# Another order of the first layer's attention units, with the output units starting on the other half of K

## The chip, the cores and the metric

The kernel runs on one core of a Trainium2 chip. The metric is the time on the device in microseconds. Three runs of the kernel before took 2024.71 to 2028.53 us, median 2028.3 us. The engines are named as in the profile: PE is TensorE's matmul stream, DVE is VectorE, ACT is ScalarE, POOL is GpSimd and SP is SyncE, which issues nearly all transfers.

## The reference, cut to what matters

Two transformer layers on 256 tokens of width 2048, all in float32. The change touches the first layer's attention only:

```python
proj = h @ w_in                      # h: modulated norm of x; 3904 columns
dq, dk, dv, q_lat, kv_lat, k_pe = split(proj, (1024, 1024, 1024, 512, 256, 64))
o_diff = diff_attention(rope(dq), rope(dk), dv, lam)      # 8 heads, two softmaxes each
o_diff = rmsnorm(o_diff, g_diff_sub) * (1 - lambda_init)
q  = rmsnorm(q_lat) @ w_q_b;  kv = rmsnorm(kv_lat) @ w_kv_b
o_mla = mla_attention(q, kv, rope(k_pe))                  # 8 heads, one softmax each
x = x + gate_m * (concat([o_diff, o_mla]) @ w_out)
h = modulate(rmsnorm(x, g_norm_ffn), shift_f, scale_f)    # then the feed-forward part
```

The shifts, scales and gates are `silu(c) @ w_ada + b_ada`, a product of one row with a matrix of 2048 x 12288.

## The kernel before, in words

**Units and pairs.** Every large product is cut into units of 512 (or 384, 320) output columns, and a unit into pairs of K tiles (2 x 128 rows). One pair is one transfer of 512 KB into one of five `raw` slots, a rounded copy by ACT (`whi`, line 1685), a remainder by DVE (`wlo`, line 1897), and 12 matmuls on PE: eight with `whi` (lines 1550 and 1551) and four with `wlo` (line 1555). Sums of a unit stand in two of four PSUM banks `g`. `run` (line 522) writes the pairs and prepares weights three pairs ahead; `whi` and `wlo` have four buffers each.

**The dots.** The product with `w_ada` is not on PE: DVE multiplies a tile of 512 KB with the row and sums it (line 1902, "dot" below). The tiles come through the same five slots. `fill` (line 457) puts a dot into the program wherever its planner, a table of assumed durations, sees DVE with time to spare. After the attention two more slots are added.

**The attention.** The first halves of K of the six `w_in` units have been computed and parked in `part` (in the tensor `region`) before the latent columns. Then the loop at line 1069 runs through the table `order1` (line 604). An entry `("h", i)` is the second half of K of unit i (0, 1: queries; 2, 3: keys; 4, 5: values), four pairs; `half_unit` (line 1033) adds the parked part on DVE. An entry `("l", i)` is `latent_units` (line 1043): two pairs for the queries and one for keys and values of latent heads 2i and 2i+1. Heads are generators in a queue `bg`: `diff_head` (line 825) and `mla_two` (line 897, two latent heads, scores of both together). Up to four of them are advanced between the pairs. A differential head 0 to 3 needs units 0, 2 and 4, a head 4 to 7 needs units 1, 3 and 5.

**What comes out.** Finished heads are normalised and turned into the K tiles of the output product: `mla_end(p)` (line 983) makes one K pair of two latent heads, `diff_end(j)` (line 881) two K pairs of four differential heads, after an inverse root by 11 small DVE instructions. The rows of `w_out` are rolled on the host, so that K tiles 0 to 7 belong to the latent heads and 8 to 15 to the differential ones. The latent K tiles take the place of the latents and can be written only when the last latent unit is done. `diff_end` is put into the queue behind everything else, after the loop. `spread` (line 640) makes the gate's rows.

**The output units.** `u_out[0]` and `u_out[1]` run their first four pairs, then `u_out[0]` its other four (lines 1105 to 1107); then the queue is drained, and `u_out[1]`, `u_out[2]`, `u_out[3]` follow, 32 pairs in all. `reload` (line 1097) has POOL load x (2.1 MB) when the queue is empty. The products are multiplied by the gate on DVE (line 2110) and added to x. The feed-forward part starts with an inverse root over all of x and matmuls at line 1581.

Of the kernel before, what the change touches and what calls it, by code (L numbers as in the profile page):

```python
# [152 lines left out]
def program(nc, a, out):  # L153
    with ExitStack() as ctx:
        build(nc, ctx, a, out)


def build(nc, ctx, a, out):
    def sb(name, shape, dt=F32, scope=ctx):
        return scope.enter_context(nc.sbuf_tensor(name, shape, dt))  # L160
# [8 lines left out]
    lhsA = Lhs(sb("lhsA_hi", [P, 16, 256], F32R), sb("lhsA_lo", [P, 16, 256], F32R), 16)  # L169
# [53 lines left out]
    region = sb("region", [P, 11264], F32, early)  # L223
# [4 lines left out]
    lamv = rowv[:, 0:256].rearrange("p (a b) -> p a b", a=4)  # L228
    red = [region[:, 10784:10864], region[:, 10864:10944]]
    gt = region[:, 0:2048]  # L230
    part = [region[:, 1024 * i:1024 * i + 1024].rearrange("p (t d) -> p t d", t=2) for i in range(6)]
    omla = region[:, 2048:4096].rearrange("p (t d) -> p t d", t=2)
    odiff = [region[:, 4096 + 1024 * j:5120 + 1024 * j].rearrange("p (t d) -> p t d", t=2) for j in range(2)]
    vm = region[:, 6144:8192].rearrange("p (t d) -> p t d", t=2)
# [58 lines left out]
    def mark(kind):  # L293

        engine, s = signal[kind]
        count[kind] = count.get(kind, 0) + 1
        latest[engine] = (s, count[kind])
        return latest[engine]

    def fence():  # L300
        return list(latest.values())
# [62 lines left out]
    def tile_of(name, k, c0):  # L364
        at, n = tile_at(name, ROWS.get(name, D), k, c0)
        return a[name][at:at + 2 * P * n].rearrange("(p x) -> p x", p=P)

    def units(us, row=0, native=False):
        built = []
        for w, c0, n, K, lhs in us:  # L370
            k_off, K = K if isinstance(K, tuple) else (0, K)
            u = dict(n=n, K=K, lhs=lhs, tiles=[], k_off=k_off, pairs=list(range(K // 2)))
            for k0 in range(0, K, 2):
                u["tiles"].append(len(plan))
                plan.append((tile_of(w, row + k_off + k0, c0), n, native))
            built.append(u)
        return built
# [4 lines left out]
    pairs, used_up, fetched = {}, {}, {}  # L382
# [103 lines left out]
    def pump(n=1, width=2, idle=False):  # L486
        for _ in range(n):
            fill()
            moved, again = False, True
            while again:  # L490
                again, live = False, 0
                for g in list(bg):
                    if live < width or g in started:
                        started.add(g)
                        live += 1
                        if soon(g, SLACK):
                            again = advance(g) or again
                moved = moved or again
            if idle and not moved:
                held = [g for g in bg if g in started and waiting.get(id(g))]  # L500
                held.sort(key=lambda g: max([due[m] for m in waiting[id(g)][1]] + [0.0]))
                for g in held:
                    if advance(g):
                        break
# [96 lines left out]
    u_h0 = units([("w_in", 512 * i, 512, (0, 8), lhsA) for i in range(6)])  # L601
    u_lat = units([("w_in", 3072, 512, 16, lhsA), ("w_in", 3584, 320, 16, lhsA)])
    u_in, u_q = {}, []
    order1 = (("h", 2), ("h", 3), ("l", 0), ("h", 0), ("l", 1), ("h", 4), ("l", 2), ("l", 3), ("h", 1), ("h", 5))
    for kind, i in order1:
        if kind == "h":
            u_in[i], = units([("w_in", 512 * i, 512, (8, 8), lhsA)])
        else:
            u_q.extend(units([("w_q_b", 384 * i, 384, 4, lhs_q), ("w_kv_b", 512 * i, 512, 2, lhs_kv)]))
    u_out = units([("w_out", 512 * i, 512, (0, 8), lhsA) for i in range(2)])  # L610
    for u, v in zip(u_out, units([("w_out", 512 * i, 512, (8, 8), lhsA) for i in range(2)])):
        u["tiles"], u["pairs"] = u["tiles"] + v["tiles"], list(range(8))
    u_out += units([("w_out", 512 * i, 512, 16, lhsA) for i in range(2, 4)])
    u_f1, u_f2 = [], []
    for g in range(4):
# [190 lines left out]
    def latents_turned():  # L806
        for p in range(3):
            b = take(SB)
            lhs, c0, k0 = (lhs_q, V_QA + 2 * p, 2 * p) if p < 2 else (lhs_kv, V_KVA, 0)
            tok = turned(b, blocks_of(lat, (2 * p * P, 2 * p * P + P)), t_of["lat", 0], t_of["lat", 512])  # L810
            split_from(b, tok, 2, [vec[:, c0 + i:c0 + i + 1] for i in range(2)], lhs, k0, *lhsA.free, t_vec)
# [171 lines left out]
    def mla_end(p):  # L983
        while any(("omla", h) not in t_of for h in (2 * p, 2 * p + 1)):
            yield
        yield "pe", [t_of["omla", 2 * p], t_of["omla", 2 * p + 1]]
        T = yield from grab(TOB)
        tok = turned(T, blocks_of(omla, (2 * p * P, 2 * p * P + P)), t_of["omla", 2 * p], t_of["omla", 2 * p + 1])
        yield "act", [tok]
        split_from(T, tok, 2, ONE, lhsA, 2 * p, t_of["latents"])  # L990
# [42 lines left out]
    def half_unit(i):  # L1033
        if i < 4:
            got = run(u_in[i], width=4)
            r = take(rows)
            bg.append(g_qk(r, sum_parts(got, i, r.ap, *r.after), qT if i < 2 else kT, 4 * (i % 2),
                           0.125 if i < 2 else 1.0, ("qT" if i < 2 else "kT", i % 2)))
        else:
            j = i - 4  # L1040
            note(("dv", j), sum_parts(run(u_in[i], width=4), i, dv[:, :, 512 * j:512 * j + 512], *stage))

    def latent_units(i):
        r, ks = row_unit(u_q[2 * i], width=4)
        bg.appendleft(g_q(r, ks, i))
        par, tok = run(u_q[2 * i + 1], steps=2, width=4)
        r = take(rows)
        got = [G[2 * par + t].rearrange("p (s w) -> p s w", w=256) for t in range(2)]
        ks, kv = mark("evac"), mark("evac")
        step("evac", [(r.ap[:, t, 0:256].rearrange("p (s w) -> p s w", w=P), got[t][:, :, 0:P], 1.0) for t in range(2)],  # L1050
             tok, r.after, ks)
        step("evac", [(vm[:, t, 256 * i:256 * i + 256].rearrange("p (s w) -> p s w", w=P), got[t][:, :, P:2 * P], 1.0)
                      for t in range(2)], tok, stage, kv)
        gfree[par] = [kv]
        note(("vm", i), kv)
        bg.appendleft(g_kv(r, ks, i))
        bg.append(mla_two(i))
# [10 lines left out]
    halved = set()  # L1068
    for kind, i in order1:
        if kind == "h":  # L1070
            half_unit(i)
            halved.add(i)
            if i == 1:
                gate_free = [latest["pe"], latest["act"], latest["dve"]]
            for j in range(2):
                if i in (j, 2 + j, 4 + j) and {j, 2 + j, 4 + j} <= halved:
                    for h in range(4 * j, 4 * j + 4):
                        bg.append(diff_head(h))
        else:
            if i == 0:  # L1080
                while counts.get("lat", 0) < 2:
                    pump(1, 4, True)
                latents_turned()
                stage = fence()
            latent_units(i)
            if i == 3:
                lhsA.ready[0:4] = [None] * 4
                t_of["latents"] = latest["pe"]
                for p in range(4):
                    bg.append(mla_end(p))  # L1090
# [387 lines left out]
    for j in range(4):  # L1478
        y = take(ys)
        for b in range(3):  # L1480
# [5 lines left out]
            u, k0 = u_br[j, b], br_at[b]  # L1486
# [20 lines left out]
    for j in range(4):  # L1507
        par, tok = run(u_o2[j])
        t = mark("rows_out")
# [864 lines left out]
```

## Time and profile before

| | |
|---|---|
| three runs | 2024.71, 2028.53, 2028.3 us |
| profiled execution | 2027.03 us, its span 2025.2 us |
| busy in the span | PE 95%, DVE 65%, ACT 46%, POOL 6% |
| granted clock, whole span | 0.98 |
| loop over `order1` and output units | about 219 to 496 us of the span |

A matmul's end is modelled in these profiles, so a time for several matmuls is best read from start to start. Where rows follow each other without idle time, their durations overlap a little; two dots in a row take 2.3 us, not 2.44.

### The profile page before, as it was taken

How to read it: one execution, taken by the hardware profiler on the slowest of the kernel's cores; microseconds unless marked ns; L12 is line 12 of the kernel's file. 1: busy time of each engine (PE TensorE's matmuls, PEld its weight loads, DVE VectorE, ACT ScalarE, POOL GpSimd, SP SyncE). 2: the span in 40 equal slices, each digit the busy share in tenths (PEclk: the TensorE clock that was granted, in tenths of full speed). 3: DMA queues.
4: the chain of work that ended last, by engine and by line, in shares of the span. 5: the costliest groups of instructions: out<-in, count | busy, mean ns of one | idle time of the engine just before them, and what ended most of it. 6: DMA issues, size and time to landing. Idle time of an engine off the chain costs nothing.

```text
span 2025.2 us, 24834 instructions
## 1 busy us (share of the span) xinstructions
PE 1930.6 (95%) x9250; PEld 1608.7 (79%) x9250; DVE 1308.6 (65%) x2056; ACT 941.6 (46%) x1437; POOL 129.7 (6%) x94
## 2 busy tenths in 40 slices
PE   6699999778899999999999999989999999999999
PEld 3278788556788888888888889889998888888887
DVE  3788888979788555555555556668666555555554
ACT  2455466524544344344434454456455544444442
POOL 0000000001000110110010022010000010100000
PEclk9899999889899999999999999999999999999999
DMA  9998686878799555555555545534545465655644
GB/s 348 368 391 339 232 282 215 292 255 326 274 321 319 196 206 186 191 188 189 186 196 187 187 167 198 189 113 158 170 151 180 147 205 190 191 190 189 198 178 176
DMA packets 128968, 448.83 MB, mean 222 GB/s; under 512 B 14288, under 2 KB 14544, under 8 KB 128336
## 3 DMA queue, kind: packets, MB, share of 16 engines
q1 hardware_dynamic: 124928, 433.74, 61.5%
q0 software_dynamic: 1568, 7.34, 1.0%
q10 hardware_dynamic: 2352, 6.17, 0.8%
q8 instruction: 73, 1.20, 0.2%
q14 instruction: 47, 0.39, 0.1%
HBM read 443.00 MB, written 4.19 MB: 221 GB/s over the span
## 4 chain that ended last, share of the span: by engine, by line
PE 90%; DVE 5%; DMA 2%; issue 1%; ACT 1%; POOL 0%; ACTq 0%; SPq 0%; DVEq 0%; POOLq 0%
PE g L1550 27%; PE g L1555 27%; PE g L1551 27%; PE pT L1574 1%; DVE raw L1902 1%; PE g L1566 1%; PE pS L1574 1%; DMA region<-in_mem 1%; PE pO L1626 1%; DMA raw<-in_w_ada 1%; DVE wlo L1897 1%; PE pT L1587 0%; PE pS L1644 0%; DMA raw_wide<-in_w_ada 0%; PE pS L1594 0%
## 5 line engine op out<-in xcount | busy, mean ns | idle before, releaser
L1897 DVE TENSOR_TENSOR wlo<-raw,whi 128x1024 fp32r<-128x1024 f32 (+3 forms) x553 | 659.2, 1198 | 519.4 <-ACT whi L1685 486.6
L1685 ACT ACTIVATE whi<-raw 128x1024 fp32r<-128x1024 f32 (+3 forms) x553 | 554.7, 1007 | 663.7 <-PE g L1555 572.3
L1550 PE MATMUL g<-whi,lhsA_hi 128*128 128x512 f32 (+4 forms) x1840 | 701.1, 383 | 40.0 <-issue 14.6
L1551 PE MATMUL g<-whi,lhsA_lo 128*128 128x512 f32 (+4 forms) x1840 | 687.9, 376 | 0.0
L1555 PE MATMUL g<-wlo,lhsA_hi 128*128 128x512 f32 (+4 forms) x1840 | 465.2, 375 | 3.2 <-DVE wlo L1897 3.1
L1550 PEld LDWEIGHTS g<-whi,lhsA_hi 128*128 128x128 f32 x1840 | 349.7, 190 | 98.7 <-issue 37.6
L1551 PEld LDWEIGHTS g<-whi,lhsA_lo 128*128 128x128 f32 x1840 | 350.1, 190 | 51.6 <-issue 0.5
L1555 PEld LDWEIGHTS g<-wlo,lhsA_hi 128*128 128x128 f32 x1840 | 339.4, 190 | 58.4 <-DVE wlo L1897 3.7
L1550 PE MATMUL g<-whi,lhsF_hi 128*128 128x512 f32 x512 | 200.9, 392 | 0.0
L1551 PE MATMUL g<-whi,lhsF_lo 128*128 128x512 f32 x512 | 199.4, 389 | 0.0
L1902 DVE SCALAR_TENSOR_TENSOR raw<-raw,srow 128x1024 f32<-128x1024 f32 x145 | 174.8, 1227 | 6.6 <-DMA raw<-in_w_ada 6.3
L1897 DVE TENSOR_TENSOR wlo<-region,whi 128x1024 fp32r<-128x1024 f32 (+1 forms) x99 | 122.8, 1248 | 85.8 <-ACT whi L1685 77.1
L1685 ACT ACTIVATE whi<-region 128x1024 fp32r<-128x1024 f32 (+1 forms) x99 | 102.1, 1036 | 124.1 <-PE g L1555 121.1
L1555 PE MATMUL g<-wlo,lhsF_hi 128*128 128x512 f32 x512 | 137.0, 390 | 0.0
L1555 PEld LDWEIGHTS g<-wlo,lhsF_hi 128*128 128x128 f32 x512 | 96.2, 188 | 20.1
L1550 PEld LDWEIGHTS g<-whi,lhsF_hi 128*128 128x128 f32 x512 | 96.2, 188 | 19.9 <-issue 0.2
L1551 PEld LDWEIGHTS g<-whi,lhsF_lo 128*128 128x128 f32 x512 | 96.2, 188 | 19.7 <-issue 0.2
L2287 POOL TENSOR_TENSOR region<-region,tmp 128x512 f32<-128x512 f32 x36 | 60.6, 1705 | 700.2 <-DVE tmp L2110 689.4
L1550 PE MATMUL g<-whi,lhsY_hi 128*128 128x512 f32 x128 | 50.2, 392 | 0.0
L1551 PE MATMUL g<-whi,lhsY_lo 128*128 128x512 f32 x128 | 49.9, 390 | 0.0
L1550 PE MATMUL g<-whi,yz_hi 128*128 128x512 f32 x128 | 49.8, 389 | 0.0
L1551 PE MATMUL g<-whi,yz_lo 128*128 128x512 f32 x128 | 49.8, 389 | 0.0
(265 smaller groups left out, 1497.7 us busy)
## 6 DMA issues: line engine op xcount, KB each, us to landing
raw<-in_w_ff SPq DMA_DIRECT2D x185, 512.0 KB, 4.2
raw<-in_w_in SPq DMA_DIRECT2D x159, 512.0 KB, 4.2
raw<-in_w_ada SPq DMA_DIRECT2D x145, 512.0 KB, 5.3
region<-in_w_ff SPq DMA_DIRECT2D x71, 512.0 KB, 4.3
raw<-in_w_out SPq DMA_DIRECT2D x60, 512.0 KB, 5.4
raw<-in_w_in SPq DMA_DIRECT2D x80, 384.0 KB, 3.1
region<-in_w_ada SPq DMA_DIRECT2D x36, 512.0 KB, 6.0
region<-in_w_in SPq DMA_DIRECT2D x17, 512.0 KB, 10.1
```

The source lines that it names most:

```text
L1550: eng.matmul(o, p.xh[:, kk, t * P:t * P + P], h, start=p.first and kk == 0, stop=False)
L1551: eng.matmul(o, p.xl[:, kk, t * P:t * P + P], h, start=False, stop=False)
L1555: ins = eng.matmul(p.banks[t][:, 0:n], p.xh[:, kk, t * P:t * P + P], p.lo[:, kk * n:kk * n + n], start=False, stop=p.last and kk == 1)
L1566: ins = eng.matmul(p.banks[t][:, 0:n], p.xh[:, kk, t * P:t * P + P], p.raw[:, kk * n:kk * n + n], start=p.first and kk == 0, stop=p.last a ...
L1574: ins = eng.transpose(b.ap[:, i * P:i * P + P], src, ident)
L1626: ins = eng.matmul(o[:, dh * r:dh * r + dh], pt[:, 256 * i + P * r:256 * i + P * r + P], vals[:, i, v0:v0 + dh], start=i == 0, stop=i == 1)
L1685: eng.activation(p.hi, p.raw, ACT.Copy).then_inc(p.hi_done[0], 1)
L1897: eng.tensor_tensor(p.lo, p.raw, p.hi.bitcast(F32), ALU.subtract).then_inc(p.lo_done[0], 1)
L1902: eng.scalar_tensor_tensor(out=x, in0=x, scalar=0.5, in1=srow[:, D // 2 * (i % 2):D // 2 * (i % 2) + D // 2], op0=ALU.mult, op1=ALU.mult, ...
L2287: eng.tensor_tensor(xc, xc, tm[:, :], ALU.add).then_inc(t[0], 1)
```

## The change

The table `order1` is another one: differential heads 0 to 3 have their last unit third (`h` 2) instead of sixth, heads 4 to 7 theirs eighth (`h` 3) instead of tenth, and latent units 2 and 3 come last. The parked parts change places in `region`, so that the two that lie where the gate's rows go (parts 5 and 3) are used up when `gate_free` is taken. Units 0 and 1 of the output product begin with K tiles 8 to 15 (differential) and end with 0 to 7 (latent); the other two are as before.

```diff
-    part = [region[:, 1024 * i:1024 * i + 1024].rearrange("p (t d) -> p t d", t=2) for i in range(6)]
+    part = [region[:, 1024 * i:1024 * i + 1024].rearrange("p (t d) -> p t d", t=2) for i in (3, 5, 4, 1, 2, 0)]
...
-    order1 = (("h", 2), ("h", 3), ("l", 0), ("h", 0), ("l", 1), ("h", 4), ("l", 2), ("l", 3), ("h", 1), ("h", 5))
+    order1 = (("h", 4), ("h", 0), ("l", 0), ("h", 2), ("l", 1), ("h", 1), ("h", 5), ("h", 3), ("l", 2), ("l", 3))
...
-    u_out = units([("w_out", 512 * i, 512, (0, 8), lhsA) for i in range(2)])
-    for u, v in zip(u_out, units([("w_out", 512 * i, 512, (8, 8), lhsA) for i in range(2)])):
-        u["tiles"], u["pairs"] = u["tiles"] + v["tiles"], list(range(8))
+    u_out = units([("w_out", 512 * i, 512, (8, 8), lhsA) for i in range(2)])
+    for u, v in zip(u_out, units([("w_out", 512 * i, 512, (0, 8), lhsA) for i in range(2)])):
+        u["tiles"], u["pairs"], u["k_off"] = u["tiles"] + v["tiles"], [4, 5, 6, 7, 0, 1, 2, 3], 0
...
-            if i == 1:
+            if {3, 5} <= halved and i in (3, 5):
                 gate_free = [latest["pe"], latest["act"], latest["dve"]]
```

PE's program shows what the planner makes of it at the end of the attention. In the kernel before, this is what follows the first four pairs of `u_out[0]` and of `u_out[1]`: the last three differential heads (pT from `probs` is a head's turned probabilities, pS its scores, pO its values), two steps of the gate's rows (`rot`), the first turned output of `diff_end` and the next pair of `u_out[0]`.

```order
L1594 MATMUL pS<-region 128x256 x4
L1626 MATMUL pO<-region,pt 128x128 x4
L1574 MATMUL pT<-cst,probs 128x128 x4
L1594 MATMUL pS<-region 128x256 x4
L1626 MATMUL pO<-region,pt 128x128 x4
L1574 MATMUL pT<-cst,probs 128x128 x4
L1587 MATMUL pT<-rot,cst 128x512
L1626 MATMUL pO<-region,pt 128x128 x4
L1574 MATMUL pT<-cst,probs 128x128 x4
L1587 MATMUL pT<-rot,cst 128x512
L1626 MATMUL pO<-region,pt 128x128 x4
L1574 MATMUL pT<-cst,region 128x128 x4
```

In the changed kernel the last pair of the last latent unit is followed by 32 such rows without one pair among them: four differential and four latent heads (the two rows at lines 1604 and 1609 are scores of two latent heads), and everything that ends them. These are the last twelve before the first pair of `u_out[0]`.

```order
L1626 MATMUL pO<-region,pt 128x128 x4
L1574 MATMUL pO<-cst,region 128x128 x4
L1574 MATMUL pT<-cst,probs 128x128 x8
L1626 MATMUL pO<-region,pt 128x128 x4
L1574 MATMUL pT<-cst,probs 128x128 x4
L1626 MATMUL pO<-region,pt 128x128 x8
L1574 MATMUL pT<-cst,region 128x128 x4
L1574 MATMUL pO<-cst,region 128x128 x4
L1587 MATMUL pT<-rot,cst 128x512
L1574 MATMUL pT<-cst,region 128x128 x4
L1574 MATMUL pO<-cst,region 128x128 x4
L1587 MATMUL pT<-rot,cst 128x512
```

What moved: in the kernel before, eight pairs of output units stand among the last eight heads, and four more among the rows of `diff_end`; now all 32 stand behind the heads.

On DVE, this stands in the kernel before around the splits of the differential K pairs (`lhsA_lo` with `vec`): dots at line 1902, the scaling by the norm at line 2071, one remainder at line 1897. The first of the four differential splits stands ahead of it.

```order
L1902 SCALAR_TENSOR_TENSOR raw,small<-raw,srow 128x1024 x3
L2071 TENSOR_TENSOR region<-region,small 128x512 x2
L1929 SCALAR_TENSOR_TENSOR lhsA_lo<-pO,vec,lhsA_hi 128x256 x2
L1937 TENSOR_SCALAR rot<-cst,small 128x128 x4
L1897 TENSOR_TENSOR wlo<-raw,whi 128x1024
L1902 SCALAR_TENSOR_TENSOR raw,small<-raw,srow 128x1024 x2
L1914 TENSOR_TENSOR mods<-small 128x4
L1917 TENSOR_TENSOR mods<-mods,vec 128x4
L1922 SCALAR_TENSOR_TENSOR mods<-mods,vec 128x4
L1929 SCALAR_TENSOR_TENSOR lhsA_lo<-pO,vec,lhsA_hi 128x256 x2
```

And this in the changed kernel, from the end of the second inverse root on:

```order
L1937 TENSOR_SCALAR rot<-cst,small 128x128 x4
L2071 TENSOR_TENSOR region<-region,small 128x512 x2
L1929 SCALAR_TENSOR_TENSOR lhsA_lo<-pT,vec,lhsA_hi 128x256 x2
L1929 SCALAR_TENSOR_TENSOR lhsA_lo<-pO,vec,lhsA_hi 128x256 x2
L1902 SCALAR_TENSOR_TENSOR raw,small<-raw,srow 128x1024 x4
L1937 TENSOR_SCALAR rot<-cst,small 128x128 x4
L1929 SCALAR_TENSOR_TENSOR lhsA_lo<-pO,vec,lhsA_hi 128x256 x2
L1929 SCALAR_TENSOR_TENSOR lhsA_lo<-pT,vec,lhsA_hi 128x256 x2
L1897 TENSOR_TENSOR wlo<-raw,whi 128x1024
```

What moved: both inverse roots and both scalings now stand ahead of the first of these splits, and behind all latent heads, because `diff_end` is queued last, although the outputs of differential heads 0 to 3 are complete long before. In the kernel before, the four latent K pairs were split first and had pairs of `u_out` behind them.

## Rows read from the trace of the kernel before

**Rows 1.** Stretches: length; busy PE, PEld, DVE, ACT, POOL; clock, DMA share, GB/s.

```profile
244.00:343.00 99.00, 99.00 (x551) 83.47 (x550) 83.15 (x167) 67.42 (x167) 0.00 (x0) 1.00 0.72 243
343.00:412.00 69.00, 54.31 (x274) 41.35 (x272) 64.52 (x152) 36.05 (x103) 0.00 (x0) 0.88 0.77 273
412.00:440.00 28.00, 19.47 (x62) 14.33 (x63) 24.88 (x54) 6.33 (x11) 0.84 (x1) 0.77 0.67 225
440.00:496.00 56.00, 55.59 (x243) 45.51 (x242) 47.97 (x64) 22.06 (x29) 10.67 (x6) 0.99 0.98 373
384.00:412.00 28.00, 18.52 (x78) 12.71 (x76) 24.70 (x69) 13.84 (x48) 0.00 (x0) 0.70 0.58 197
```

**Rows 2.** Waits of PE and of SP's queue, 343 to 441 us: total, times, longest.

```profile
PE g L1550 <- DVE lhsA_lo L1929: 10.1, 4, 4.5
SPq L1529 <- DVE raw L1902: 56.2, 35, 8.1
```

**Rows 3.** DVE's instructions by line, 343 to 412 us: count, busy us, mean ns, idle before.

```profile
L1902 DVE SCALAR_TENSOR_TENSOR raw<-raw,srow 128x1024 f32<-128x1024 f32 x24 | 28.8, 1219 | 0.3 <-DMA raw<-in_w_ada 0.3
L1897 DVE TENSOR_TENSOR wlo<-raw,whi 128x1024 fp32r<-128x1024 f32 x10 | 12.2, 1222 | 0.1
L1937 DVE TENSOR_SCALAR rot<-cst,small 128x128 f32<-128x128 f32 x12 | 2.6, 280 | 0.0
L1929 DVE SCALAR_TENSOR_TENSOR lhsA_lo<-pT,lhsA_hi 128x256 fp32r<-128x256 f32 x4 | 1.5, 418 | 0.0
L2071 DVE TENSOR_TENSOR region<-region,small 128x512 f32<-128x512 f32 x2 | 1.3, 686 | 0.0
L2104 DVE TENSOR_TENSOR region<-g,region 128x512 f32<-128x512 f32 x2 | 1.3, 684 | 0.0
```

**Rows 4.** PE in order of time: start us, us, instruction, idle time before it.

```profile
342.16 1.07 PE L1555 MATMUL g<-wlo,lhsA_hi 128*128 128x512 f32 x4
343.95 1.89 PE L1604 MATMUL pS<-region 128*128 128x256 f32 x8
345.78 1.14 PE L1609 MATMUL pS<-hn_sq,region 64*128 64x256 f32 x8
...
390.68 2.09 PE L1594 MATMUL pS<-region 64*128 64x256 f32 x8
...
412.10 0.47 PE L1550 MATMUL g<-whi,lhsA_hi 128*128 128x512 f32 x1 [2.07 <-DVE lhsA_lo L1929]
...
416.14 1.42 PE L1587 MATMUL pT<-rot,cst 128*128 128x512 f32 x2
...
440.93 0.39 PE L1550 MATMUL g<-whi,lhsA_hi 128*128 128x512 f32 x1
...
505.12 1.20 PE L1581 MATMUL pS<-region 128*128 128x128 f32 x4 [9.54 <-issue]
```

**Rows 5.** The chain that ended last: start us, us, what (three dots with their reads).

```profile
364.48 3.44 DVE raw L1902 x6
```

**Rows 6.** DVE in order of time: an inverse root, and a late dot.

```profile
403.39 0.16 DVE L1860 TENSOR_SCALAR small<-small 128x8 f32<-128x8 f32 x1
...
405.39 0.17 DVE L1872 SCALAR_TENSOR_TENSOR small<-small 128x8 f32<-128x8 f32 x1
...
497.38 1.23 DVE L1902 SCALAR_TENSOR_TENSOR raw<-raw,srow 128x1024 f32<-128x1024 f32 x1 [2.12 <-DMA raw<-in_w_ada]
```

**Rows 7.** Transfers from 440 to 497.4 us: packets, bytes, mean rate.

```profile
DMA packets 5649, 21.45 MB, mean 374 GB/s; under 512 B 611, under 2 KB 611, under 8 KB 5455
```

**Rows 8.** Transfers' size and median us to landing, 343 to 412 us.

```profile
raw<-in_w_out SPq DMA_DIRECT2D x9, 512.0 KB, 5.2
```

**Rows 9.** The same from 420 to 450 us.

```profile
raw<-in_w_out SPq DMA_DIRECT2D x5, 512.0 KB, 8.7
```

**Rows 10.** POOL in order of time: the load of x, and what waited for it.

```profile
436.23 0.84 POOL L2276 DMA_DIRECT2D region<-in_x  x1 [435.79 <-DVE lhsA_lo L1929]
447.86 3.61 POOL L2287 TENSOR_TENSOR region<-region,tmp 128x512 f32<-128x512 f32 x2 [10.78 <-DMA region<-in_x]
```

## The prediction, made before the changed kernel was run

> **What bounds the kernel now.** I read the stretches first, then the waits in the one that is not full, then DVE's groups, then the transfers. [rows 1] show three regimes around the change. From 244 to 343 us PE is busy throughout at full clock (2.4 GHz, granted 1.00) while DVE has 16 us to spare of 99: PE is the bound, and moving work about gives nothing there. From 343 to 440 us PE has holes and a lower clock, while DVE is busy 64.5 of 69 us and 24.9 of 28: DVE is the bound. SP's queue waits for DVE as well, because each dot holds a slot [rows 2]. From 440 to 496 us PE is full again, with the transfers at 98%: the bound is PE with the transfers right behind it. The proof of "right behind" is the last dot before the final gate product, which sat 2.1 us for its data at 497.4 us, when PE had been done since 495.6 (505.12 less 9.54) [rows 4, 6].
>
> So the question is what the change does to the middle regime, and whether the third one can still follow.
>
> **Start of the tail.** In the kernel before, the last pair of the last attention unit ends at 343.1 us (the first row of [rows 4] with what lies behind it). In the changed kernel the same number of pairs stands ahead of the last latent unit's end. Of the other PE work, one step of scores of two latent heads (343.95 to 346.9 us, 2.9 us [rows 4]) and two turned outputs (0.44 us each at full clock) are not ahead any more, and one differential head's scores more are (2.09 us at half clock, so about 1.05). PE was the bound there, so this counts: 343.1 - 2.9 - 0.9 + 1.1 = 340.4 us.
>
> **The tail without pairs.** In both kernels eight heads are unfinished at that point. Before, eight pairs stood among them and the first pair that needs a differential split began at 412.1 us [rows 4]. Now none stands among them, so PE is free; but PE was not the bound. I take DVE's work of 343 to 412 us and change what the order changes: 64.5 us; ten remainders were in it, one is now (9 x 1.15 = 10.3 less); 24 dots, now 23 (1.15 less); 12 rows of `rot`, now 8 (0.8 less); the parked sum and one rope (2.4 less); one inverse root more (403.39 to 405.39 and its last instruction, 2.1) and one scaling (1.2) [rows 3, 5, 6]; splits and output copies, 0.5 more. That is 53.6 us, and 1.1 for the first scores, 54.7. A dot is 1.15 from start to start (3.44 for three [rows 5]).
>
> To this come DVE's own waits. Before they were 4.5 us in 69 (69 less 64.5), with six of the last eight heads under cover of other DVE work. Now the last four heads are latent, scored two at a time, and DVE stands behind a chain: maximum, exponential on ACT, turn, copy, values, output, turn, split, and each only when the one bank for turns is free again. From 384 to 412 us, where heads ran without pairs, the clock was 0.70, mostly at 1.2 GHz, and DVE was busy 24.7 of 28 [rows 1]. At full clock I count three such stops, 8 us in all; at 1.2 GHz the two steps of latent scores cost 5.8 instead of 2.9 us each and the turns and values double, 14 us. I take 11, nearer to neither, since the clock was mixed. The first output pair then begins at 340.4 + 54.7 + 11 = 406.1 us, with 4.5 and 14 as bounds: 400 to 409.
>
> Before it began at 412.1; so the tail is about 6 us shorter. But before, twelve pairs were done or under way by 440 us, eight of them in this stretch. Now all 32 stand behind it.
>
> **The 32 output pairs.** The undisturbed pace: from 440.93 to 495.6 us there are 20 pairs, 2.73 us each [rows 4]. The first twelve (units 0 and the half of 1, on five slots): 12 x 2.73 = 32.8; two turned outputs of `diff_end(1)`, 0.9; two steps of `rot`, 1.7; a first pair that begins in the low clock, 1.3 (412.10 to 416.14 us is 4.0 [rows 4]). Then the load of x. It is 2.1 MB, 5.6 us at the 374 GB/s of [rows 7]. Before, it was issued at 436.2 and landed at 447.9 us [rows 10], and weights took 8.7 us to land around it instead of 5.2 [rows 8, 9]; PE did not feel it, since it had been slow just before and three prepared pairs were waiting. Now it falls after about the sixth of 32 pairs in a row, with DVE just ahead of PE (11 remainders and 18 dots belong to these twelve pairs, 33 us, with splits and `rot` 39 us against PE's 37). I put 3 of the 5.6 us on the path; the bounds are 0 and 5.6. Sum 39.7: unit 0 ends at 445.8 us. Then 20 pairs as before, 54.6, and 1 us because they start with empty slots: 501.4 us.
>
> The transfers by themselves: 62 tiles for remainders and dots, three for the next stage, less five in the slots, is 60 x 0.524 MB, with x 33.6 MB, 90 us at 374 GB/s [rows 7]. 406 + 90 = 496 us. They can follow, but with 5 us in 95 to spare, which is why a lost microsecond is not given back.
>
> The Trainium skill, DMA: Bandwidth & Descriptors, section Issuing engines are not separate DMA queues, says that transfers started by any engine run on the same 16 DMA engines and interleave. Here the trace agrees: the load of x goes through POOL, and the weights of SP's queue landed 3.5 us later around it [rows 8, 9]. The same page's Specifications give about 358 GB/s from HBM for a core; the trace does not agree, with 374 over 57 us [rows 7]. By that figure the 33.6 MB would take 94 us and the last tile would land at 500 us instead of 496, which is still not behind PE's 501.4.
>
> **The sum.** Last output pair 501.4 against 495.6: +5.8. The late dot ahead of the last gate product should be as late as before. The changed order has one dot more ahead of the feed-forward part (82 against 81) and one fewer at its start, where PE waits for a scale that the dots make: -1.1. In all +4.7 us. The profiled execution took 2027.0 us, so 2031.7 by its measure; it lies 1.3 us under the median of the runs, so 2033.0 by theirs. Everything behind the start of the feed-forward part is the same program. About 4 us (0.2%) either way is what a measurement can tell from no change, so this is only just a loss.
>
> **Rivals.**
> A. The gains and losses cancel. The tail's waits are at their full-clock value of 8 us (3 less than taken) and the load of x is hidden but for 1 us (2 less): -0.3, so 2028.0. For it: the heads' chain has slack on PE now. Against: the low clock wherever heads ran alone [rows 1].
> B. It ends faster. The wait for turned latent outputs is really gone: PE waited 10.1 us in four places for `lhsA_lo` in the tail and twice more for `whi` there [rows 2]; if DVE packs the tail as densely as before (4.5 us of waits, first pair at 399.6) and the 32 pairs run without any disturbance (36.7 for the first twelve, no last microsecond), the last pair ends at 490.9, less 1.1: -5.8, 2022.5. It decides in the tail: the first output pair must begin before about 402 us. Against it: the transfers would then need 96% of the time.
> C. It ends much slower. The tail is at 1.2 GHz throughout (14 us), x costs all of its 5.6 us, and the shortage of slots in the first twelve pairs costs 3 more: +3 +2.6 +3 on +4.7 is +13.3, 2041.6.
> D. The reordered units lose where PE is full: a unit's heads are not ready in time and PE gets holes before 340 us. [rows 1] show 16 us of room on DVE and none on PE; each hole would count in full. I give it no time of its own; it widens the upper side by 3.
>
> Chances: the forecast and C together, slower by over 0.2%: 0.48, of which C and D 0.15. A, within 0.2%: 0.33. B: 0.19. The range leaves out half of B's far side and the end of C with D: 2022 to 2044; the forecast's own is 2029 to 2037.
>
> **What would show it.** Right: no pair for some 65 us after 340 us, clock near 0.7 there, DVE busy over 80% of it; the first output pair at 402 to 409 us; a slow landing of weights 15 to 25 us later and DVE or ACT waiting for them; matmuls of line 1581 at 507 to 514 us; then everything shifted by one constant. Wrong: PE idle before 340 us (D); a tail under 60 us (B); or a first output pair before the differential roots, which the order excludes. If the shift at line 1581 is there but the end is not shifted, the later stages absorb it, and my step "the same program behind" fails.

## The result, and the profile after

| | before | after |
|---|---|---|
| median, us | 2027.26 (22 runs, 2023.51 to 2031.68) | 2030.89 (22 runs, 2026.69 to 2034.20) |
| span of the profiled execution, us | 2025.2 | 2030.5 |
| last pair of the last latent unit ends, us | about 343.1 | 340.0 |
| first output pair that needs a differential split, us | 412.1 | 403.5 |
| last output pair ends, us | 495.6 | 503.5 |
| matmuls of line 1581 begin, us | 505.12 | 511.19 |

The ratio of after to before is 1.0017, 95% interval 1.0011 to 1.0024: 3.5 us slower (2.2 to 4.9), of 4.7 forecast. The two profiled executions differ by 5.3 us.

The stretches of the kernel after, which answer to [rows 1] (length; busy PE, PEld, DVE, ACT, POOL; clock, DMA share, GB/s):

```profile
244.00:340.00 96.00, 96.00 (x539) 80.99 (x537) 81.38 (x168) 63.66 (x160) 0.00 (x0) 1.00 0.70 235
340.00:404.00 64.00, 38.87 (x192) 28.71 (x191) 55.94 (x148) 31.00 (x103) 0.00 (x0) 0.77 0.61 220
404.00:440.00 36.00, 33.45 (x138) 26.42 (x137) 31.05 (x55) 11.50 (x15) 0.85 (x1) 0.94 0.85 312
440.00:503.50 63.50, 60.82 (x260) 49.50 (x258) 52.46 (x70) 25.24 (x32) 9.53 (x6) 0.97 0.94 360
```

From 244 us to about 340 us PE is full in both. The heads' stretch is 64 us long, holds no pair, and DVE is busy 55.9 us of it. Behind it PE is busy 94.3 of 99.5 us: better filled than in the kernel before, but with all 32 output pairs still to do.

PE of the kernel after in order of time, for [rows 4]: the last pair of the heads' stretch, the two steps of latent scores, the first output pair, the gap, the last output pair, line 1581, the first feed-forward pair that waits for its scale.

```profile
338.96 1.07 PE L1555 MATMUL g<-wlo,lhsA_hi 128*128 128x512 f32 x4
...
362.01 3.62 PE L1604 MATMUL pS<-region 128*128 128x256 f32 x8
365.56 1.93 PE L1609 MATMUL pS<-hn_sq,region 64*128 64x256 f32 x8
...
371.60 3.11 PE L1604 MATMUL pS<-region 128*128 128x256 f32 x8
374.64 1.13 PE L1609 MATMUL pS<-hn_sq,region 64*128 64x256 f32 x8
...
403.53 1.40 PE L1550 MATMUL g<-whi,lhsA_hi 128*128 128x512 f32 x1
...
455.33 0.50 PE L1550 MATMUL g<-whi,lhsA_hi 128*128 128x512 f32 x1 [2.67 <-ACT whi L1685]
...
502.43 1.07 PE L1555 MATMUL g<-wlo,lhsA_hi 128*128 128x512 f32 x4
511.19 1.22 PE L1581 MATMUL pS<-region 128*128 128x128 f32 x4 [7.69 <-DVE region L2127]
...
544.01 0.77 PE L1550 MATMUL g<-whi,lhsA_hi 128*128 128x512 f32 x1 [6.08 <-DVE lhsA_lo L2003]
```

The same feed-forward pair of the kernel before:

```profile
538.26 0.76 PE L1550 MATMUL g<-whi,lhsA_hi 128*128 128x512 f32 x1 [7.51 <-DVE lhsA_lo L2003]
```

It is 5.75 us later after the change, and everything behind it is later by about that: the first sum of the feed-forward part on POOL begins at 646.82 us instead of 641.49.

DVE of the kernel after, 340 to 404 us, by line, for [rows 3]:

```profile
L1902 DVE SCALAR_TENSOR_TENSOR raw<-raw,srow 128x1024 f32<-128x1024 f32 x23 | 26.9, 1219 | 0.0
...
L2077 DVE TENSOR_REDUCE small<-pS 128x2 f32<-128x512 f32 x4 | 2.7, 686 | 2.7 <-PE pS L1609 2.7
L2071 DVE TENSOR_TENSOR region<-region,small 128x512 f32<-128x512 f32 x4 | 2.6, 682 | 0.0
L1897 DVE TENSOR_TENSOR wlo<-raw,whi 128x1024 fp32r<-128x1024 f32 x2 | 2.4, 1222 | 1.1 <-ACT whi L1685 1.1
...
L1937 DVE TENSOR_SCALAR rot<-cst,small 128x128 f32<-128x128 f32 x8 | 1.7, 279 | 0.0
```

23 dots, two remainders, four scalings, eight rows of `rot`, as forecast but for one remainder.

The weights behind the stretch (SP's queue in order of time; then ACT, which makes the first part of each weight):

```profile
438.05 0.33 SPq L1529 DMA_DIRECT2D raw<-in_w_ada  x1
439.19 0.33 SPq L1529 DMA_DIRECT2D raw<-in_w_out  x1
444.68 0.33 SPq L1529 DMA_DIRECT2D raw<-in_w_ada  x1
450.69 1.95 SPq L1529 DMA_DIRECT2D raw<-in_w_out  x3
```

```profile
442.28 1.06 ACT L1685 ACTIVATE whi<-raw 128x1024 fp32r<-128x1024 f32 x1 [5.58 <-DMA raw<-in_w_out]
...
454.22 1.06 ACT L1685 ACTIVATE whi<-raw 128x1024 fp32r<-128x1024 f32 x1 [4.87 <-DMA raw<-in_w_out]
```

The load of x was issued at 431.86 us. A weight landed late around it (ACT stood 5.58 us for it), its remainder was late, the dots queued behind that remainder on DVE were late, and so the five slots came free late: between 439.19 and 450.69 us SP issued one transfer. PE lived on prepared pairs, then waited 2.67 us and ran its next pair, from 455.33 us on, partly at the low clock.

One sum holds both kernels. The feed-forward scale needs the 160th dot. It ends at 531.3 us before and at 537.0 after; the stretch from 340 us to there, first of the kernel before, then of the one after:

```profile
340.00:531.30 191.30, 157.99 (x729) 126.37 (x727) 168.62 (x322) 86.73 (x181) 11.51 (x7) 0.89 0.80 290
```

```profile
340.00:537.00 197.00, 158.95 (x717) 127.58 (x717) 166.72 (x318) 87.74 (x181) 10.38 (x7) 0.88 0.77 285
```

DVE has 1.9 us less to do and stands idle 30.3 instead of 22.7 us: +7.6 - 1.9 = +5.7 us, the whole shift. That is bookkeeping, not yet a cause.

### The profile page after: what moved, and what is told of

Same layout as the page of the kernel before. It is cut to its first block, busy times and chain, and to the rows that moved or that the text cites. A ratio compares the mean times of both kernels' runs of the same rounds, so it can differ in the third digit from the quotient of the medians.

```text
span 2030.5 us, 24842 instructions
## 1 busy us (share of the span) xinstructions
PE 1934.7 (95%) x9250; PEld 1612.7 (79%) x9250; DVE 1308.4 (64%) x2056; ACT 941.9 (46%) x1437; POOL 128.5 (6%) x94
## 4 chain that ended last, share of the span: by engine, by line
PE 84%; DVE 6%; DMA 6%; ACT 2%; issue 1%; POOL 0%; ACTq 0%; SPq 0%; DVEq 0%; POOLq 0%
PE g L1550 26%; PE g L1551 25%; PE g L1555 25%; DMA raw<-in_w_out 3%; DVE raw L1902 2%; PE pT L1574 1%; PE pS L1574 1%; PE g L1566 1%; DMA region<-in_mem 1%; DVE wlo L1897 1%; ACT whi L1685 1%; DMA raw<-in_w_ada 1%; PE pO L1626 1%; PE pS L1644 0%; PE pO L1574 0%
```

## The experiments

All ratios are to the kernel before, timed beside it on one chip, with 95% intervals.

**Each half alone.** swap_only is the kernel before with `u_out` of the changed one; order_only is the changed kernel with

```
-    u_out = units([("w_out", 512 * i, 512, (8, 8), lhsA) for i in range(2)])
-    for u, v in zip(u_out, units([("w_out", 512 * i, 512, (0, 8), lhsA) for i in range(2)])):
-        u["tiles"], u["pairs"], u["k_off"] = u["tiles"] + v["tiles"], [4, 5, 6, 7, 0, 1, 2, 3], 0
+    u_out = units([("w_out", 512 * i, 512, (0, 8), lhsA) for i in range(2)])
+    for u, v in zip(u_out, units([("w_out", 512 * i, 512, (8, 8), lhsA) for i in range(2)])):
+        u["tiles"], u["pairs"] = u["tiles"] + v["tiles"], list(range(8))
```

> The kernel before, with only the first two output units changed: they run over K tiles 8 to 15 first, then 0 to 7. With the old order of the attention units the split of the first differential half is then the last thing but one, so no output pair can stand among the unfinished heads. Theory 1 (the loss comes from the output pairs that stood among the heads and now all stand behind them, whatever the order of the units): this kernel is about as slow as the changed one or slower, ratio 1.001 to 1.004, first output pair 404 to 412 us, last output pair 502 us or later. Theory 2 (the order of the units is what loses, the K tiles are innocent): ratio 0.999 to 1.001.

> The changed kernel with only the output units put back: they run over K tiles 0 to 7 first. With the latent units last, only some 4 to 6 output pairs can stand among the latent heads at the end. Theory 1 (loss by pairs put behind the heads): less of the loss remains than in the changed kernel, ratio to before 0.999 to 1.001, last output pair 499 to 502 us. Theory 2 (the order of the units loses by itself): ratio 1.0015 or more.

> The same kernel as order_only, for a second profiled execution, since the first one (2024.5 us) was the fastest of its eleven and its profile can't show where the median of 2029.4 comes from. If the order of the units alone loses 3 to 4 us, the ratio stays at 1.001 to 1.003, and a profile near the median shows the place: low clock in the stretch 340 to 440 us with the output pairs between the latent heads. If the first result was scatter, the ratio falls to 0.9995 to 1.001.

swap_only: 1.0007 (0.9998 to 1.0016). order_only: 1.0019 (1.0010 to 1.0029), and again 1.0015 (1.0006 to 1.0024). The order of the units alone loses what both halves lose together; the swap alone costs nothing that can be told from zero. Theory 1, that the pairs put behind the heads are the loss, has the worse of it: swap_only has them all behind too (first output pair at 403.3 us, last ending at 508.4, 5 us later than in the changed kernel), and its ratio lies in theory 2's range. Its interval ends at 1.0016, inside theory 1's range, so a small loss by the swap is not excluded. In its trace the late pairs cost nothing, because its 160th dot is done at 507.3 us and no feed-forward pair waits. Of order_only2:

```profile
404.51 0.47 PE L1550 MATMUL g<-whi,lhsA_hi 128*128 128x512 f32 x1 [2.30 <-DVE lhsA_lo L1929]
...
418.85 0.77 PE L1550 MATMUL g<-whi,lhsA_hi 128*128 128x512 f32 x1 [10.90 <-DVE lhsA_lo L1929]
...
512.33 1.07 PE L1555 MATMUL g<-wlo,lhsA_hi 128*128 128x512 f32 x4
```

PE stands 10.9 us before a pair that needs a differential split; the last pair ends at 513.4 us, and again nothing waits for the scale. The two debts are exchanged: pairs done late with all dots made, or pairs early with 6 or 7 dots owed.

**The load of x, later.**

```
     def reload():
-        while len(bg) > 1:
-            yield
+        yield
...
-    bg.append(reload())
...
     first_out = run(u_out[0], steps=2, width=6, lo_i=4)
     drain(width=4)
+    bg.append(reload())
+    drain(width=4)
```

> The changed kernel with one thing moved: the 2.1 MB load of x is issued only when the first output unit has been summed, some 15 us later, so that it doesn't fall into the first pairs behind the heads while only five weight slots are in the ring. Theory 1 (the load costs 3 to 5 us there, since nothing is prepared ahead): ratio to before 0.9995 to 1.0008, that is 2 to 4 us under the changed kernel, and the gap in the weights near 449 us is gone. Rival (the total of the bytes ahead of the last output pair is what counts, and the load only moves the gap): no change against the changed kernel within 1 us, ratio 1.0012 to 1.0024.

1.0040 (1.0028 to 1.0053): neither theory; it is worse. Issued at 447.02 us, the load makes a PE gap of 3.33 us where there was one of 2.67. Now the first additions to x wait for it too: POOL's, at line 2287, begin only at 460.02 us, after 12.15 us of waiting for x, and a gate product waits for POOL. The disturbance goes where the load goes. That accounts for little of the 4.7 us that this kernel loses against the changed one: the two profiled executions differ by 0.35 us. The rest is not located.

```profile
466.03 0.50 PE L1550 MATMUL g<-whi,lhsA_hi 128*128 128x512 f32 x1 [3.33 <-ACT whi L1685]
```

```profile
464.31 0.69 DVE L2110 TENSOR_TENSOR tmp<-g,region 128x512 f32<-128x512 f32 x1 [0.55 <-POOL region L2287]
```

**No dots in the heads' stretch.**

```
-            if raw_free[i] is None or (state["hold"] and adas[0][0] >= 20):
+            if raw_free[i] is None or state.get("tail") or (state["hold"] and adas[0][0] >= 20):
```

The flag is set behind the loop over the attention units and cleared behind the first output pair.

> The changed kernel with the dots of the row products switched off from the end of the latent units' pairs until the first output pair; they are computed later, ahead of the feed-forward part, so the work is the same and only its place differs. Theory 1 (VectorE bounds the tail, and everything before the feed-forward part has too little room behind it): the first output pair comes 20 us or more earlier, at 375 to 385 us, but the 20 dots are then due among the output pairs, the end is not earlier: ratio to before 1.002 to 1.010. Rival (the tail is bound by the chain of each head, not by VectorE's work): the first output pair moves by under 10 us and the total is worse by the full 20 dots, ratio 1.010 or more.

1.0104 (1.0089 to 1.0120), in the rival's range, at the edge of theory 1's. Of tail_few, the last pair ahead of the heads, the first output pair, the second, and the two feed-forward pairs that wait; then the stretch between the first two rows:

```profile
334.97 1.07 PE L1558 MATMUL g<-wlo,lhsA_hi 128*128 128x512 f32 x4
...
388.62 1.42 PE L1553 MATMUL g<-whi,lhsA_hi 128*128 128x512 f32 x1
...
397.45 0.79 PE L1553 MATMUL g<-whi,lhsA_hi 128*128 128x512 f32 x1
...
529.83 0.77 PE L1553 MATMUL g<-whi,lhsA_hi 128*128 128x512 f32 x1 [13.80 <-DVE lhsA_lo L2006]
...
555.18 0.77 PE L1553 MATMUL g<-whi,lhsA_hi 128*128 128x512 f32 x1 [14.23 <-DVE lhsA_lo L2006]
```

```profile
336.00:388.60 52.60, 32.22 (x191) 23.30 (x191) 29.23 (x94) 30.42 (x103) 0.00 (x0) 0.88 0.10 35
```

From the end of the last pair to the first output pair the heads take 52.6 us (388.62 less 336.04), against 63.5 in the changed kernel. So neither account holds alone. DVE has 26.4 us less to do (29.2 instead of 55.7), and the stretch is only 10.9 us shorter: a chain through the heads is left that takes 52.6 us with DVE idle for 23 of them. But 10.9 us did come back, 0.4 us for each us of dots, which a stretch set by the chain alone would not give. (The pair itself begins 14.9 us earlier; 4.0 of these were there at the start of the stretch. The granted clock was 0.88 in it instead of 0.77, and may have a part in the 10.9.) Taken out here, the dots are missing later: two feed-forward pairs wait 13.8 and 14.2 us.

**Nine microseconds off DVE in the stretch.**

```
+                n_dot += 1
+                c0, cw = D // 2 * (i % 2), 64 if 101 <= n_dot <= 108 else D // 2
-                eng.scalar_tensor_tensor(out=x, in0=x, scalar=0.5, in1=srow[:, D // 2 * (i % 2):D // 2 * (i % 2) + D // 2],
+                eng.scalar_tensor_tensor(out=x[:, 0:cw], in0=x[:, 0:cw], scalar=0.5, in1=srow[:, c0:c0 + cw],
```

> The changed kernel with eight dots of VectorE cut from 1024 to 64 columns (numbers 101 to 108, which run in the stretch of heads without pairs, 340 to 404 us), so the row products of those columns are not the reference's; every transfer and wait stays. It takes 8 x 1.15 = 9 us from VectorE alone. Theory 1 (VectorE's work bounds the stretch, and what is saved there goes through to the end, since PE and the transfers then have no slack behind it): first output pair 396 to 399 us, end 5 to 9 us below the changed kernel, ratio to before 0.9975 to 0.9995. Rival (the chain of each head bounds the stretch, VectorE has 8 us idle there already): first output pair not before 402 us and end within 2 us of the changed kernel, ratio 1.0008 to 1.0022.

0.9996 (0.9986 to 1.0005): 4.3 us under the changed kernel's ratio. The value lies between the two ranges, the interval reaches into theory 1's and not into the rival's, and the first output pair is where theory 1 had it. Of less_dve:

```profile
336.78 1.07 PE L1555 MATMUL g<-wlo,lhsA_hi 128*128 128x512 f32 x4
...
397.07 1.42 PE L1550 MATMUL g<-whi,lhsA_hi 128*128 128x512 f32 x1
```

```profile
340.00:530.00 190.00, 153.28 (x708) 121.94 (x709) 157.29 (x315) 85.65 (x178) 10.38 (x7) 0.91 0.78 291
```

The stretch of heads is 59.2 us long (397.07 less 337.85) instead of 63.5: half of the 9.4 us comes back there. The 160th dot is done at 530.0 us, 7.0 earlier, DVE being idle 32.7 us, 2.4 more (2.2 of the 7.0 us are an earlier start of the stretch in this execution). A microsecond of DVE in this stretch is worth about a half; with the errors of both ratios, 0.2 to 0.7. tail_few gives 0.4 for the stretch. The two agree: DVE's work lengthens the stretch by less than half of its own length, because the rest of it falls into gaps of the heads' chain. That the steps of a head wait behind dots in DVE's queue is the likely reason; no run isolates it from the clock, which was 0.82 in less_dve's stretch.

**Clock held up in the stretch.** Ahead of each long wait of PE, and at most 14 at a time:

```
+            if kind == "warm":
+                _, bank, after, n = s
...
+                for i in range(n):
+                    eng.matmul(bank[:, 0:256], qnT[:, 0, 0:P], knT[:, 0, :], start=True, stop=True)
```

> The changed kernel with some 150 matmuls of 256 columns more on PE in the stretch of heads without pairs, put ahead of its long waits, into a sum bank that nobody uses then; no other instruction moves. It holds the granted clock up. Theory 1 (VectorE's work bounds, PE's clock matters only in the two steps of latent scores and what follows them): granted clock 0.9 or more in 340 to 404 us instead of 0.76, first output pair 1 to 4 us earlier, ratio to before 1.0000 to 1.0012. Rival A (low clock is what the change costs): 5 us or more earlier, ratio 0.9995 or less. Rival B (the extra matmuls stand in the way of the heads more than the clock gives): later than 405 us, ratio 1.002 or more.

1.0126 (1.0112 to 1.0140): rival B, and far beyond its lower end of 1.002. Of warm:

```profile
L1559 PE MATMUL g<-region 128*128 128x256 f32 x254 | 56.6, 379 | 0.0
```

```profile
422.96 0.79 PE L1570 MATMUL g<-whi,lhsA_hi 128*128 128x512 f32 x1
```

```profile
340.00:424.00 84.00, 82.05 (x447) 69.92 (x448) 56.61 (x149) 31.35 (x104) 0.00 (x0) 1.00 0.48 167
```

The clock was 1.00 throughout, and the first output pair began 19.4 us later. The experiment was mis-sized: the 127 matmuls (two records each) kept PE busy for 56.6 us, not for the 15 meant, PE was busy 82 of 84 us, and so it became the bound itself. The rest of PE's work in the stretch shrank from 38.9 us to about 25 (82.05 less 56.6), which is what the clock is worth to PE; what it is worth to the heads stays unmeasured.

**Splitting early, and cover.** early_end queues `diff_end(0)` as soon as six differential units are done:

```
+            if len(halved) == 6:
+                lhsA.ready[4:8] = [None] * 4
+                bg.appendleft(diff_end(0))
```

slices adds to that output units 0 and 1 in slices:

```
+    for i, k0 in ((0, 8), (1, 8), (0, 0), (1, 0), (0, 12), (0, 4), (1, 12), (1, 4)):
+        v, = units([("w_out", 512 * i, 512, (k0, 4), lhsA)])
+        u_out[i]["tiles"] += v["tiles"]
...
+    for lo_i in (0, 2):
+        for u in u_out[0:2]:
+            run(u, steps=2, width=4, lo_i=lo_i, hi_i=lo_i + 2)
```

> The changed kernel with the split of differential heads 0 to 3 queued as soon as these heads can be finished, ahead of the latent heads, and not behind them; so one or two output pairs of K tiles 8 to 11 stand in the stretch of heads, and 30 behind it. Theory 1 (pairs behind the stretch cost what they don't get as cover): 1 to 3 us better than the changed kernel, ratio to before 1.0003 to 1.0015. Rival (VectorE's work is one sum up to the scale of the feed-forward part, and where the pairs stand doesn't matter): within 1 us of the changed kernel, 1.0013 to 1.0022.

> early_end with the first two output units run by slices of four K tiles, in turn: K 8 to 11 of both, K 0 to 3 of both, then the rest. Eight output pairs then stand among the heads, as in the kernel before, though the latent units are last. Theory 1 (the latent units at the end lose, whatever stands among their heads, since what bounds is VectorE's work and what it waits for up to the scale of the feed-forward part): ratio 1.0008 to 1.002. Rival (what the change loses is the cover, eight pairs among the heads): ratio 0.9995 to 1.0005, first feed-forward pair as early as in the kernel before.

early_end: 1.0016 (1.0007 to 1.0024), the rival's value, no gain to be seen, though the interval covers most of theory 1's range too. slices: 1.0033 (1.0020 to 1.0046), worse than either said. Of early_end, then of slices:

```profile
507.94 2.07 PE L1582 MATMUL pS<-region 128*128 128x128 f32 x8 [11.24 <-DVE region L2128]
...
541.11 0.76 PE L1551 MATMUL g<-whi,lhsA_hi 128*128 128x512 f32 x1 [7.43 <-DVE lhsA_lo L2004]
```

```profile
499.69 2.08 PE L1584 MATMUL pS<-region 128*128 128x128 f32 x8 [7.61 <-DVE region L2130]
...
544.33 0.76 PE L1553 MATMUL g<-whi,lhsA_hi 128*128 128x512 f32 x1 [18.93 <-DVE lhsA_lo L2006]
```

The last output pair ended at 496.7 us in the one and at 492.1 in the other, 7 and 11 us before the changed kernel's. In slices all of it is lost in front of line 1581 and of the scale, where it waits 18.9 us: its early remainders ran in place of dots, of which 142 were done at 500 us instead of the changed kernel's 152. early_end had as many dots done by then (152), lost 4 of its 7 us all the same, and the 2.9 us that are left at the feed-forward pair (541.11 against 544.01) don't show in its median. In both, PE's progress was not the thing to look at.

**Latent units not last.** The changed order, with latent units 2 and 3 ahead of units 5 and 3, and `u_out` of the kernel before:

```
-    order1 = (("h", 4), ("h", 0), ("l", 0), ("h", 2), ("l", 1), ("h", 1), ("h", 5), ("h", 3), ("l", 2), ("l", 3))
+    order1 = (("h", 4), ("h", 0), ("l", 0), ("h", 2), ("l", 1), ("h", 1), ("l", 2), ("l", 3), ("h", 5), ("h", 3))
```

> The changed order of the first layer's units with one thing different: the latent units 2 and 3 stand ahead of units 5 and 3 and not behind them, so the last heads are differential ones; the output units run over K tiles 0 to 7 first, as in the kernel before. The early part of the order (4, 0, latent 0, 2, latent 1, 1) is the changed one. Theory 1 (it is the latent units at the end that lose, because their heads end late and everything on the output side waits for VectorE after them): within 0.1% of before, ratio 0.999 to 1.0005, last output pair 494 to 500 us. Rival (the other order of the differential units loses, or anything that moves the stretch): ratio 1.001 or more.

1.0008 (0.9999 to 1.0017). This lies between theory and rival, and its interval overlaps those of order_only. It points to the latent units at the end as the greater part of the loss, and doesn't show it. Its trace also warns against taking the 160th dot for a law. That dot is done at 536.4 us, nearly as late as in the changed kernel (537.0), but the feed-forward pair begins 3.2 us behind it, at 539.64 us, and not 7.0: in the changed kernel a remainder that waits 4.4 us for ACT stands between the two.

**A faster one?** The kernel before, with `diff_end(0)` queued first and output units 0 and 1 run as K 0 to 7, then 8 to 11, then 12 to 15:

```
+    bg.appendleft(diff_end(0))
     bg.append(spread(0, gate_free))
-    bg.append(diff_end(0))
...
+    for i, k0, K in ((0, 0, 8), (1, 0, 8), (0, 8, 4), (1, 8, 4), (0, 12, 4), (1, 12, 4)):
+        v, = units([("w_out", 512 * i, 512, (k0, K), lhsA)])
+        u_out[i]["tiles"] += v["tiles"]
```

> The kernel before with the split of differential heads 0 to 3 queued ahead of the last heads, and the first two output units in slices (K 0 to 7 of both, K 8 to 11 of both, then 12 to 15), so that four more output pairs are ready while VectorE ends the last heads and PE waited 2.1 and 4.5 us there for splits. Theory 1 (VectorE bounds the stretch: with more to overlap it idles a little less): 1 to 3 us faster than before, ratio 0.9985 to 0.9995. Rival (PE's waits there cost nothing since VectorE's sum is the same): ratio 0.9995 to 1.0005.

1.0003 (0.9993 to 1.0012): the rival's value. But the edit did not do what it was meant to. PE still waited 10.6 us in four places for `lhsA_lo` between 343 and 452 us (10.1 in four places up to 441 us before, [rows 2]), so what such waits are worth stays unmeasured. No kernel of this study beat the one before.

## Why the prediction came out right

The forecast was +4.7 us; the profiles differ by 5.3 and the medians by 3.6 us. The 2033.0 us had 1.3 us in it for the distance of the profiled execution from the median of three runs; from the median of 22 it is 0.2 us. And +0.17% is by its size a case of rival A (within 0.2%, 0.33), not of "slower by over 0.2%" (0.48), though the interval (1.0011 to 1.0024) says that it is a loss. By its own steps:

- *Start of the tail, 340.4 us.* 340.0. PE was full from 244 us until then, so rival D is out.
- *The tail without pairs, first output pair at 406.1 us.* 403.5. DVE's work was right (54.7 forecast, 55.9 of the 64 us busy). The waits were 8.1 us, not 11: the value for the full clock, though the clock was 0.77 and the first step of latent scores took 5.5 us. But the model under it, DVE's work plus a fixed wait, is only half true. By it the stretch without dots would take about 39 us (54.7 less 26.4, plus 11); tail_few took 52.6, with 23 us of waits. The waits are not a constant: they are the gaps of the heads' chain that dots do not fill, and the sum came out because 23 dots fill most of them.
- *The first twelve pairs, 39.7 us.* The twelfth ended at 444.5 us, 41 us after the first began. The load of x showed itself as forecast, weights taking 8.4 us to land around it, but PE paid for it later than I had put it. (In [rows 9]'s stretch of the kernel before, the tiles of `w_ada` still landed in 5.1 us at the median, so 3.5 us later was true of `w_out` alone there; in the changed kernel, from 432 to 452 us, both were slow, 8.9 and 8.4 us.)
- *The 20 pairs behind, 54.6 + 1 us.* This term was mis-sized: 59.0 us. The two gaps of slots at 439 to 451 us reached PE only at 455.33 us. So the last output pair ended 7.9 us later than before (5.8 forecast).
- *-1.1 us for one dot more ahead of the feed-forward part.* 154 dots against 153 stood ahead of line 1581, and the wait for the scale fell from 7.51 to 6.08 us. From the last pair to line 1581 another 1.8 us came back (7.69 instead of 9.54 of waiting), which I had not counted; a low clock right behind it took about 1 us away again.
- *The same program behind.* The shift is 5.75 us at the first waiting feed-forward pair, 5.33 on POOL at 646.82 us and 5.3 at the end.

The number is near by luck as well: against the forecast the stretch of heads ended 2.6 us early, the pairs took 4.7 us longer, and 1.8 us came back that were in no term.

Of the rivals, B's condition (first output pair before about 402 us) was missed by 1.5 us, and its end by far: even at 397 us, less_dve only reaches the time of before. (Its transfers would have needed 90 of 91.3 us, 99% and not 96%.) C's full 1.2 GHz did not come about (0.77). A's terms held for the tail (8 us of waits) but not for the pairs.

The reason behind the number was less good than the number. I made the whole sum along PE, from pair to pair, with the dots as a correction of 1.1 us at its end. The experiments speak against that: early_end and slices move the last output pair by 7 and 11 us, and their medians gain nothing. The account that fits the traces best is that the kernel's two debts, 32 pairs and 160 dots, are paid from one purse of DVE time and slots, and that the later of the two counts. No run isolates either, and order_mid shows that what stands behind the last dot matters as well.

What stays open: why the changed order leaves DVE idle 7.6 us more. 5.6 us of it lie ahead of 405 us, where the last heads are latent, scored two at a time, and DVE waited 2.7 us for their scores and 2.0 us for a turned output. order_mid's median agrees with that within its error and no more. What the clock contributes was not isolated.

## What to carry to other kernels

When several kinds of work are due before one point (here pairs and row products before the feed-forward scale), price an edit by the time at which the last of them is complete, not by the progress of the busiest engine: pairs that move forward by taking the place of dots give nothing. An engine that is 87% busy in a stretch is not yet its bound. Take its filler away and see how much of it comes back: here 10.9 of 26.4 us did, so the stretch was a chain with filler in its gaps, and the filler neither set it nor was free. And see in the trace that the wait which an experiment was to remove is gone: in before_slices it was not, and its time says nothing of what the wait costs.

## What the runs showed of the hardware

The granted clock of PE stayed at 1.00 (2.4 GHz) over 84 us of heads when its waits were filled with matmuls of no use, where it had been 0.77; but they took 56.6 us of PE themselves, 0.45 us each for 256 columns, four times what I had put down. Their operands were plain 32-bit floats; the four matmuls of 512 columns at line 1555, with rounded operands, take 1.07 us together. And the same program differs between executions by several microseconds, mostly by the clock: from 219 to 244 us it was 0.86 in the profiled execution of the changed kernel and 1.00 in that of order_only, with the same instructions there. The two were 0.25 us apart at 229.7 us and 3.6 us at 244.4 us, 0.7 of it by a longer wait of PE (3.58 against 2.90 us), and the stretch of heads began 3.6 us apart. The first profile of order_only took 2024.5 us against a median of 2029.4, and this is 3.6 of the 4.9. A single profile of this kernel doesn't decide about 0.2%.
